# The third weight slot of an attention block's entry, taken in row form and turned back behind four tiles

## The reference

```python
u = rmsnorm_2(h, g_pre_mix[i])
proj = jnp.einsum('bsd,de->bse', u, w_in[i])          # 1024 -> 2304
qa, ka, va, qb, kb, vb = [proj[..., offs[j]:offs[j + 1]] for j in range(6)]
o_a = rmsnorm_2(windowed_gqa_sink(qa, ka, va, rel_bias_table, sink_a[i]), g_out_a[i])
o_b = rmsnorm_2(dilated_mixture(qb, kb, vb, rel_bias_table), g_out_b[i])
mix = jnp.einsum('bse,ed->bsd', jnp.concatenate([o_a, o_b], axis=-1), w_o[i])
h = h + rmsnorm_2(mix, g_post_mix[i])
...                                                   # MLP and a gated product follow
```

## Time and profile before

| what | value |
|---|---|
| median of 3 runs | 1992.37 us (1992.18 to 1992.89) |
| the profiled execution's own time | 1991.88 us |
| its span, first to last instruction | 1990.0 us |
| PE busy | 1973.6 us (99% of the span) |
| DVE busy | 1327.0 us (67%) |
| ACT busy | 989.3 us (50%) |
| mean granted clock of TensorE | 0.999 of full speed |
| moved by DMA | 369.18 MB, mean 186 GB/s |

### The profile page before, as it was taken

One profiled execution on the slowest core, in us unless ns is written; L12 is line 12 of the kernel. 1 busy time (PEld: TensorE's weight loads), 2 busy tenths in 40 slices (PEclk: granted clock), 3 DMA queues, 4 the chain that ended last, 5 costly groups with the idle time before them and its releaser, 6 DMA issues.

```text
span 1990.0 us, 25898 instructions
## 1 busy us (share of the span) xinstructions
PE 1973.6 (99%) x10542; PEld 1693.5 (85%) x10542; DVE 1327.0 (67%) x1632; ACT 989.3 (50%) x1379; POOL 108.8 (5%) x211
## 2 busy tenths in 40 slices
PE   9999999999999999999999999999999999999998
PEld 7888998878888888888889887888888888978886
DVE  6757778457676674766669765576666666777665
ACT  5445465344444544544545644444454445754444
POOL 1012000000000000100310000000010101110001
PEclk9999999999999999999999999999999999999999
DMA  8565455534665556465654564456645664445552
GB/s 289 176 232 181 149 185 197 190 127 170 214 209 191 176 184 221 171 201 191 226 175 158 171 208 152 155 187 211 217 164 179 235 231 143 137 153 183 189 192 105
DMA packets 241141, 369.18 MB, mean 186 GB/s; under 512 B 6775, under 2 KB 171927, under 8 KB 241022
## 3 DMA queue, kind: packets, MB, share of 16 engines
q1 hardware_dynamic: 236000, 352.34, 52.4%
q0 software_dynamic: 4528, 14.85, 2.4%
q10 hardware_dynamic: 494, 0.32, 0.1%
HBM read 366.28 MB, written 1.08 MB: 185 GB/s over the span
## 4 chain that ended last, share of the span: by engine, by line
PE 98%; ACT 1%; DVE 1%; issue 0%; POOL 0%; DMA 0%; DVEq 0%; POOLq 0%; ACTq 0%
PE ps L1727 23%; PE ps L1747 22%; PE ps L1986 20%; PE ps L1729 12%; PE ps L1837 6%; PE ps L1717 2%; PE ps L1716 2%; PE ps L1718 2%; PE ps L1796 2%; PE ps L1816 1%; PE ps L1927 1%; PE ps L1772 1%; PE ps L2156 1%; PE ps L1869 0%; PE ps L2133 0%; PE ps L2181 0%
## 5 line engine op out<-in xcount | busy, mean ns | idle before, releaser
L1134 DVE TENSOR_TENSOR w_lo<-raw,w_hi 128x1024 fp32r<-128x1024 f32 x638 | 751.8, 1221 | 333.3 <-ACT w_hi L717 331.0
L717 ACT ACTIVATE w_hi<-raw 128x1024 fp32r<-128x1024 f32 x638 | 639.9, 1053 | 306.5 <-PE ps L1747 174.7
L1727 PE MATMUL ps<-u,w_hi 128*128 128x512 f32 x1968 | 470.6, 391 | 0.0
L1727 PEld LDWEIGHTS ps<-u,w_hi 128*128 128x128 f32 x1968 | 362.5, 188 | 71.5 <-issue 0.8
L1729 PEld LDWEIGHTS ps<-u,w_lo 128*128 128x128 f32 x1968 | 252.3, 191 | 9.6
L1729 PE MATMUL ps<-u,w_lo 128*128 128x256 f32 x1968 | 255.4, 283 | 0.0
L1986 PE MATMUL ps<-w_hi,u 128*128 128x512 f32 x640 | 205.0, 396 | 0.0
L1986 PEld LDWEIGHTS ps<-w_hi,u 128*128 128x128 f32 x640 | 120.2, 188 | 26.4 <-issue 1.9
L1747 PE MATMUL ps<-w_hi,h_hi 128*128 128x512 f32 x448 | 138.5, 390 | 0.0
L1747 PE MATMUL ps<-w_lo,h_hi 128*128 128x512 f32 x448 | 138.2, 390 | 0.0
L1747 PE MATMUL ps<-w_hi,h_lo 128*128 128x512 f32 x448 | 138.1, 389 | 0.0
(11 more groups left out here) (305 smaller groups left out, 2527.7 us busy)
## 6 DMA issues: line engine op xcount, KB each, us to landing
raw<-in_w_mix_in_dram SPq DMA_DIRECT2D x112, 1024.0 KB, 5.0
raw<-in_ffn_w_in_dram SPq DMA_DIRECT2D x80, 1024.0 KB, 5.1
raw<-in_ffn_w_out_dram SPq DMA_DIRECT2D x44, 1024.0 KB, 4.9
raw<-in_w_ret_out_dram SPq DMA_DIRECT2D x16, 1024.0 KB, 5.0
raw<-in_w_up_dram SPq DMA_DIRECT2D x16, 1024.0 KB, 5.4
raw<-in_w_down_dram SPq DMA_DIRECT2D x16, 1024.0 KB, 4.9
raw<-in_w_in_dram SPq DMA_DIRECT2D x9, 1024.0 KB, 5.2
raw<-in_w_lru_out_dram SPq DMA_DIRECT2D x8, 1024.0 KB, 5.0
```

The lines of the kernel that those rows point to most:

```text
L717: A(parts(n)[0][:, part], raw[i % RAW][:, part], ACT.Copy).then_inc(heads_done, 1)
L1134: V.tensor_tensor(parts(n)[1][:, part], raw[i % RAW][:, part], parts(n)[0][:, part], ALU.subtract)\
L1727: M(ps[:, bank0 + a, :], hi[:, k, P * a:P * a + P], u[:, :, k, :], start=k == 0, stop=False)
```

## The change

The third slot of the last block's attention entry is made a third slot in row form. `THREE_HEADS` gets g = 6, and with it all that the entries of g = 1 to 5 already do: `head_slot(6, 2, tt)` for both token tiles with `turn(6, 1)` in its middle, `third_copy` on ACT, the second half of `rest(B_IN + 2)` ahead of `pre_scales(6, 1)` on DVE, and `head` and `rest` of B_IN + 5 at the end of the entry. The old places of `head(B_IN + 5)` and `rest(B_IN + 5)` go. The third slot is turned back by 4 transposes after the first four tiles of B_IN + 3. Bank 7 holds the third slot's rows at that time, so B_IN + 3 goes to bank 4. The value transposes come after 12 tiles of the projection in place of 8. The order of the loads (`ORDER`) comes out the same.

```diff
-IN_BANK = (0, 1, 2, 7, 0, 1, 0, 1, 0)
+IN_BANK = (0, 1, 2, 4, 0, 1, 0, 1, 0)
...
-THREE_ROWS, THREE_HEADS = range(1, G_UP), range(1, G_UP - 1)
+THREE_ROWS, THREE_HEADS = range(1, G_UP), range(1, G_UP)
... # ACT
             projected(0)
             projected(1)
-            head(B_IN + 5)
             act.wait_ge(rel_stored, 16)
             projected(3)
... # DVE
-            rest(B_IN + 5, 0)
             dve.wait_ge(b["v_turned"], 1)
             dve.wait_ge(rel_stored, 16)
             V.tensor_copy(v_attn[:, :, 512:640], ...).then_inc(b["v_rows"], 1)
-            rest(B_IN + 5, 1)
... # PE
-            column_slot(B_IN + 2, bank(2), u_hi, u_lo)
             turn_back(G_UP - 1, (0, 1))
-            projection(0, 8)
+            projection(0, 4)
+            turn_back(G_UP - 1, (2,), 2)
+            projection(4, 12)
             pe.wait_ge(b["proj_ready"], 1)
             for tt in range(TT):
                 ins = nc.tensor.transpose(...)
             ins.then_inc(b["v_turned"], 1)
-            projection(8, 16)
+            projection(12, 16)
```

## The result

The changed kernel takes 1995.17 us (median of 21 runs, 1993.97 to 1995.80), the kernel before 1992.29 (21 runs, 1991.55 to 1993.55). The ratio is 1.0014, interval 1.0008 to 1.0020: 2.9 us slower, where 1.2 us faster was forecast. It is clear of noise and still within the 0.2% that was called "same".

What follows compares the result with a forecast made beforehand. PE, with 98% of the chain of waits, was taken to bound the kernel; 1.68 us won in the entry less 0.44 for transposes gave 1.24, so 1991.13 us from 1992.37, range 1990.3 to 1992.3.

Steps and rivals of the forecast that it cites:

- Part 1: Entry g = 6, first transposes to turning back: takes the sister entries' 20.22 us in place of 21.90, 1.68 us less.
- Part 2: Turning back of the third slot: four new transposes on PE with no work to hide them cost 0.44 us.
- Part 3: Turning back to first logits: swaps, copies and values all ready in time, nothing lost; second swap's slack 1.2 us.
- the rival: Before the first logits: second key swap late beside B_IN + 8's load, 1992.2 or 1993.9 us in all; chance 0.07.
- Part 4: Attention behind the entry: moves with PE and carries the 1.24 us through; bounds 0.8 lost and 0.2 won.
- The rule of the skill: DMA engines alternate between queues by whole packets, so packets of a 1 MB load hold up a small transfer; no size given.
- The sum: Whole kernel: 1.68 - 0.44 = 1.24 us gained, median from 1992.37 to 1991.13, called "same"; forecast's chance 0.72.
- "third" rival: Range's wording; third listed is entry g = 6 closing only its first hole, gain 0.56, 1991.8 us, chance 0.06.
- the second in its list: Attention stage takes the gain back, an earlier start only being waited off: between 1991.9 and 1992.4 us; chance 0.09.

Runs made afterwards that it cites:

- e1: Changed kernel with head and rest of B_IN + 5 back in their old places: 1992.19 us, ratio 0.9998 to the kernel before.
- e2: Changed kernel with one more wait on SP, the load of B_IN + 8 waiting for both key swaps to land: 1991.15 us, ratio 0.9994 to the kernel before.
- e5: Changed kernel with the load of B_IN + 8 issued as four DMAs of 256 KB: 1991.44 us, ratio 0.9996 to the kernel before.
- e6: Changed kernel with 11 extra identity matmuls on PE ahead of the waits of the first logits: 1993.87 us, ratio 1.0008 to the kernel before.
- e3: Changed kernel with the load of B_IN + 8 cut to its first half, 512 KB, not computing the reference: 1991.70 us, ratio 0.9998 to the kernel before.
- e7: Kernel before with an extra 768 KB load into an unread tile, issued by SP when projected(2) is done: 1992.60 us, ratio 1.0001 to the kernel before.
- e8: Changed kernel with both key swaps issued by SP directly ahead of the load of B_IN + 8, not by ACT: 1990.94 us, ratio 0.9993 to the kernel before.

## Why the prediction was wrong

**Part 1, the entry, was right.** 1.68 was forecast, 1.59 came: 20.31 in place of 20.22, with the transposes of tile 1 at 9.55. In e1, e2, e5 and e6 these are 20.20 to 20.21 and 9.45. One reading in it was wrong: the cover that was to hide POOL's longer step is not whole. In the changed kernel the transposes of tile 1 start 0.63 us after DVE's scaling and 0.37 us after the matmul in front of them, where the rhythm is 0.12 (in e2 0.64 and 0.28). So they wait for the scaling, some 0.25 us here and 0.16 in e2. This is in the sisters' 20.22 as well, so the sum had it. POOL's step took 1.54 us here and 1.46 in e2, which fits the 0.1 us by which 20.31 is above 20.20.

**Part 2 was right.** In e2, where nothing else interferes, turning back to first logits is 1683.54 - 1676.18 = 7.36 against 7.37 forecast: the transposes cost 0.43.

**Part 3 failed, at "Nothing is late, so part 3 costs nothing".** This is the step that made the forecast wrong. The swap's landing was taken as the 2.0 us of the earlier trace rows, measured on empty queues, although the same part had worked out that the load would be issued 4.6 us earlier, and the rival that this puts it a quarter us ahead of the second swap. The load was issued 0.21 us ahead of the swap, at 1679.90 and 1680.11. The term was mis-sized: 5.7 in place of 2.0. The rival's own formula then gives 1679.37 + 5.7 - 1682.58 = 2.5 us of waiting, and 2.48 was measured. The rival had the mechanism, the place and the formula of the wait; it was given 0.07, for the reason that the late transfers in the rows were three and eight times as large. e3, e5 and e7 show that this reason was the wrong one: here the small transfer's time was that of the load that it came behind (4.3 with half of it, 5.7 with all), and not that of its own size.

**A term was missing.** The rival's bill ended with the wait. PE's clock behind a standstill of 2.5 us cost 1.5 us more (e6), over a third of the 4.0 us that were lost. With both, -1.24 + 2.53 + 1.50 is 2.8.

**Part 4 was right.** The attention carries the distance through; the wait at L2145's place is 0.8 us in every profile, of before, of after and of the experiments.

**The rule of the skill.** Its direction was right: the small transfer issued behind a large one is held up by it, and less when the large one comes in pieces (3.4 against 5.7 us). The Trainium skill (DMA: Bandwidth & Descriptors, Queues, rings and completion order) puts the turn at a whole packet. If the engines take turns, a turn here was at least the 754 pieces of 1 KB that ran with the swap waiting, about 47 on each of 16 engines. No run shows that they do take turns, since order of arrival fits as well.

**The sum.** With the swap ahead of the load the kernel gives 1991.15 (e2) and 1990.94 (e8), against 1991.13 forecast. The forecast described the kernel that these two are. Of the gain over the kernel before neither ratio is sure: both intervals hold 1.0. The "about 0.2%, 4 us" that the prediction gave as what can be told from no change was too coarse for the result: 21 runs of each kernel told 2.9 us. And where its range speaks of the "third" rival, the times meant are those of the second in its list.

## What to carry to other kernels

When a change lets a load go earlier, write down for each small transfer that someone waits for which load is now in front of it, and price it at the load's landing, not at its own on an idle queue; then keep the order by issuing the small one first in the same queue, or by one wait on the queue that loads. The wait of PE of about 2.5 us cost more than itself here, since its clock fell behind it; one of 1.1 us did not cost that here. And a slack that shrinks (here 3.5 to 1.2 us) is a change of its own, even if the sum books it at nothing.

## What the runs showed that was not expected

A DMA of 64 KB issued 0.2 us behind one of 1 MB on another queue landed with it, 5.7 us after its issue in place of 2.0; the first swap, issued 0.4 us ahead of the load, was not touched (2.0). The granted clock fell to 0.51 of full speed behind 2.48 us without a matmul (0.6 us or more after PE had started again), came back some four microseconds after PE had started again, and stayed at 1.00 with 11 identity matmuls in the gap, and with a gap of 1.11 or 1.15 us.
